# A decoder step on one core: half of a page step is put inside the projection tile ahead of it

## The reference

```python
score = jnp.einsum('bqhl,bqh->bql', jax.nn.relu(s), wi)    # s = qi . ki over all cached and new keys
_, idx = lax.top_k(score, topk)                            # 256 of 2056 keys
logits = jnp.einsum('bqhd,bqkhd->bqhk', q, ks) * HEAD_DIM ** -0.5
p = jax.nn.softmax(logits)
out = jnp.einsum('bqhk,bqkhd->bqhd', p, vs)
```

## Time and profile before

| | |
|---|---|
| runs, us | 942.56, 942.96 (median), 946.93 |
| profiled execution, us | 943.09 |
| its span, us | 941.3 |
| granted TensorE clock, mean | 0.998 |
| PE busy | 926.4 us, 98% of the span |
| DVE busy | 534.3 us, 57% |
| DMA | 205.21 MB, mean 218 GB/s |

### The profile page before, as it was taken

How to read it: one execution, slowest core, us unless ns; L and a number is a source line. 1 busy time by engine, 2 the same in 40 slices (tenths; PEclk the granted TensorE clock), 3 DMA queues, 4 the chain that set the end, 5 groups by cost and what they waited for, 6 DMA issues and landing times.

```text
span 941.3 us, 20330 instructions
## 1 busy us (share of the span) xinstructions
PE 926.4 (98%) x7052; PEld 478.3 (51%) x7064; DVE 534.3 (57%) x1625; ACT 309.5 (33%) x670; POOL 270.1 (29%) x481
## 2 busy tenths in 40 slices
PE   8999999999999999999999999999999999999996
PEld 5534444444454556654564444444445555565543
DVE  6359999579952223324354699967898323332332
ACT  3122132431242456433322221334222425563312
POOL 5832222323222222312832031323232222221130
PEclk9999999999999999999999999999999999999999
DMA  9964857677867665755885175767777667666551
GB/s 323 156 216 146 280 182 254 206 274 244 272 210 243 230 224 181 266 192 194 225 244 154 63 237 212 251 226 259 247 248 247 217 226 258 211 228 239 182 193 57
DMA packets 93665, 205.21 MB, mean 218 GB/s; under 512 B 16055, under 2 KB 28566, under 8 KB 93570
## 3 DMA queue, kind: packets, MB, share of 16 engines
q0 software_dynamic: 38576, 122.63, 38.5%
q1 hardware_dynamic: 49218, 76.87, 24.8%
q10 hardware_dynamic: 5776, 4.46, 1.8%
HBM read 193.88 MB, written 10.14 MB: 217 GB/s over the span
## 4 chain that ended last, share of the span: by engine, by line
PE 81%; DVE 10%; DMA 4%; issue 2%; ACT 1%; SPq 1%; ACTq 1%; POOL 0%; POOLq 0%; DVEq 0%
PE bank L1598 35%; PE bank L1976 12%; PE bank L1652 6%; PE bank L1581 6%; DVE r L1186 5%; PE bank L1615 4%; DMA pg<-in_cache_k_dram 4%; PE bank L1885 2%; PE bank L1848 2%; PE bank L1675 2%; PE bank L1764 2%; PE bank L1706 2%; PE bank L1894 1%; DVE sel_i L1198 1%; PE bank L1801 1%
## 5 line engine op out<-in xcount | busy, mean ns | idle before, releaser
L1598 PE MATMUL bank<-wr,ht 128*128 128x512 f32 (+1 forms) x1024 | 434.3, 577 | 0.1
L1598 PEld LDWEIGHTS bank<-wr,ht 128*128 128x128 f32 x1024 | 189.9, 190 | 212.4 <-issue 200.3
L762 POOL DMA_DIRECT2D pg<-in_cache_v_dram x128 | 69.2, 541 | 157.8 <-PE bank L1652 119.9
L762 POOL DMA_DIRECT2D pg<-in_cache_k_dram x128 | 69.4, 542 | 121.1 <-PE bank L1615 101.9
L745 POOL DMA_DIRECT2D wr<-in_w_in_dram x47 | 34.7, 738 | 234.0 <-PE bank L1598 157.5
L1186 DVE TENSOR_SCALAR_CACHE_REDUCE r<-r,sel_i 128x1088 bf16<-128x1088 f32 x62 | 83.3, 1344 | 1.7
L1615 PE MATMUL bank<-pg,qbx 128*32 128x256 f32 x1024 | 63.5, 383 | 1.9 <-DMA pg<-in_cache_k_dram 1.2
L1581 PE MATMUL bank<-wr,ht 128*32 128x256 f32 (+1 forms) x1152 | 63.6, 371 | 0.0
L1652 PE MATMUL bank<-pg,rs 128*32 128x256 f32 x1024 | 61.9, 382 | 0.1
L1976 PE MATMUL bank<-wr,qt 128*128 128x512 f32 x128 | 58.4, 599 | 0.0
L1976 PE MATMUL bank<-wr,ht 128*128 128x512 f32 x128 | 57.5, 592 | 0.0
(11 more groups left out here) (275 smaller groups left out, 1108.5 us busy)
## 6 DMA issues: line engine op xcount, KB each, us to landing
pg<-in_cache_k_dram SPq DMA_DIRECT2D x128, 256.0 KB, 5.4
pg<-in_cache_k_dram POOLq DMA_DIRECT2D x128, 256.0 KB, 5.9
pg<-in_cache_v_dram SPq DMA_DIRECT2D x128, 256.0 KB, 5.4
pg<-in_cache_v_dram POOLq DMA_DIRECT2D x128, 256.0 KB, 5.8
wr<-in_w_in_dram POOLq DMA_DIRECT2D x40, 512.0 KB, 4.2
wr<-in_w_in_dram POOLq DMA_DIRECT2D x3, 2048.0 KB, 10.4
wr<-in_w_out_dram POOLq DMA_DIRECT2D x8, 512.0 KB, 4.5
wr<-in_w_out_dram POOLq DMA_DIRECT2D x2, 2048.0 KB, 9.0
```

The costliest lines, as they stand in the source:

```text
L762: pool.dma_start(PG[2 * gi + e], cache[l, bass.ds(nos[2 * gi + e], 1), :, :].rearrange("o p n -> p (o n)"))\
L1598: mm = pe.matmul(b[0:m, 0:w], HT[:, k, rt * P:rt * P + m], W[n % 2][:, k, 0:w], start=(k == 0), stop=(k == KC - 1))
```

## The change

1. Four K steps a layer are parted: K(0,1), K(0,2), K(0,3) and K(1,2). Their half u = 0 is issued inside the tile right ahead of the step (tiles 10, 11, 12 and 17), between its k = 3 and k = 4; half u = 1 stays at the step's place.
2. `take`: the count is of scores not above the threshold, the mask is made by one subtraction, and the factor -1e30 sits in the selectors; one DVE instruction over 1088 columns goes away. The steps "rep" 0 and 1 move ahead of `take`.
3. The rotations of k, row tiles 0 to 2, move from slots 16 to 18 to behind the first three "mk" steps, in slot 18.
4. ACT's key requests of layer 0 stand in slots 0, 1, 2, 3, 3, 4, 5, 5 and no longer 0, 1, 2, 2, 3, 3, 4, 5.
5. The turning of q's row tile 3 moves one slot back, and ("sg", ST) from slot 41 to slot 43.

```diff
 SELECTORS = np.concatenate([(...) for t in range(2)], 1)
-.astype(np.float32)
+.astype(np.float32) * np.float32(-BIG)
...
-        for n, s in zip((0, 1, 2, 2, 3, 3, 4, 5), KEY_STEPS[0]):
+        for n, s in zip((0, 1, 2, 3, 3, 4, 5, 5), KEY_STEPS[0]):
...
-        if name in ("kg", "qi", "q", "k") and n != s0:
+        if name in ("kg", "qi", "q", "k") and n != s0 and (name, rt) not in (("k", 0), ("k", 1), ("k", 2)):
...
-        put(at["q", rt] + 2, FRONT, ("T", "q", rt))
+        put(at["q", rt] + 2 + (rt == 3), FRONT, ("T", "q", rt))
...
-    put(s0 + 9, FRONT, ("take",))
-    put(s0 + 10, FRONT, ("rep", 0), ("rep", 1))
+    put(s0 + 9, FRONT, ("rep", 0), ("rep", 1), ("take",))
...
+            if (p, j) == (0, 0):
+                put(n, part, *[("rope", "k", rt) for rt in range(3)])
...
-    put(41, COLS, ("sg", ST))
+    put(43, COLS, ("sg", ST))
...
+PARTED = {}
+for _l in range(DEPTH):
+    for _p, _j in ((0, 1), (0, 2), (0, 3), (1, 2)):
+        _s = ("K", _l, _p, _j)
+        PARTED[[t for t in TILE_ORDER if STEPS.index(t) < STEPS.index(_s)][-1]] = _s[1:]
...
-                then(nc.vector.tensor_scalar(SC, SC, t, None, ALU.is_gt, ALU.add, accum_out=CNT))
+                then(nc.vector.tensor_scalar(SC, SC, t, None, ALU.is_le, ALU.add, accum_out=CNT))
...
-                then(nc.vector.tensor_scalar(NEED, CNT, -1.0, float(KS_), ALU.mult, ALU.add))
+                then(nc.vector.tensor_scalar(NEED, CNT, float(KS_ - 2 * HKN), None, ALU.add))
...
-                then(nc.vector.tensor_tensor(NEED, NEED, CNT2, ALU.subtract))
+                then(nc.vector.tensor_tensor(NEED, NEED, CNT2, ALU.add))
...
-                then(nc.vector.tensor_tensor(MSK, SC, eq, ALU.add))
-                nc.vector.tensor_scalar(MSK, MSK, -1.0, BIG, ALU.add, ALU.mult).then_inc(madd_ready, 1)
+                nc.vector.tensor_tensor(MSK, SC, eq, ALU.subtract).then_inc(madd_ready, 1)
...
                     for k in range(KC):
+                        if k == KC // 2 and halfway is not None:
+                            k_step(*halfway, (0,))
                         mm = pe.matmul(b[0:m, 0:w], HT[:, k, rt * P:rt * P + m], W[n % 2][:, k, 0:w],
...
-            def k_step(l, p, j):
+            def k_step(l, p, j, halves=(0, 1)):
...
-                for u in range(2):
+                for u in halves:
...
-                    project_tile(*s[1:])
+                    project_tile(*s[1:], PARTED.get(s))
...
-                    k_step(*s[1:])
+                    k_step(*s[1:], (1,) if s[1:] in PARTED.values() else (0, 1))
```

More of the change, by code:

```diff
@@ L131 @@
 SELECTORS = np.concatenate([(((_ROW // 16) % 2 == t)[:, None] & (((_ROW // TQ) % 2)[:, None] == (_ROW // NS)[None])
-                             & ((_ROW % TQ)[:, None] == (_ROW % TQ)[None])) for t in range(2)], 1).astype(np.float32)
+                             & ((_ROW % TQ)[:, None] == (_ROW % TQ)[None])) for t in range(2)], 1).astype(np.float32) * np.float32(-BIG)
 _BIT = (1 << np.arange(BITS - 1, -1, -1)).astype(np.int32)
@@ L1584, in sample_product, with project_tile @@
                 return mm
-            def project_tile(l, name, rt):
+            def project_tile(l, name, rt, halfway=None):
                 ci, w = CHUNK[name]
```

## The result

The changed kernel takes 979.26 us (median of 6, 977.02 to 985.12; the profiled execution 978.49), the one before 944.22 (median of 6, 942.56 to 946.93). The ratio is 1.0386, 95% interval 1.0365 to 1.0407: 35 us slower, where 962.4 was forecast and 968 was the upper end. The sign and the place were right, the size was not: some 14 us, the price of a lower clock, were given to a rival with a chance of 0.08.

A forecast was written before the change was run, and what follows sets the result against it. TensorE's own list was taken as the bound, with no slack; 12.6 + 9.2 + 2.4 - 4.9 = 19.3 us on 943.09 us gives 962.4 us, 2.0% slower. Own range 957 to 968 us, 80% in 953 to 968.

The forecast's parts named there:

- The mechanism of the stops: Tiles 10, 11, 12 and 17, both layers: TensorE stops inside the tile for POOL's pages, eight stops of 2 to 4 us.
- second kind: K(0,2), K(0,3): POOL's page request stands behind the weight load's wait for the whole tile; 2.3 us four times, 9.2 us.
- first kind: K(0,1), K(1,2), both layers: the whole step ahead frees POOL's pages too late for mid-tile; 2.7 to 3.8 us each, 12.6 us.
- group 0 was out of the way: K(0,2), K(0,3): SP's pages (group 0) are requested earlier, so a landing of 5.0 us was taken for POOL's pages.
- The switch: Each parted half goes in and out of the tile once more: 0.3 us, eight times, 2.4 us; bounds 0 and 0.6.
- What it gives back: Gains across both layers: late last halves 1.8, ACT's requests 1.0, the mask 0.9, the small gate 1.2; sum 4.9 us.
- the three waits: TensorE's waits at q's turning (0.98 us), the mask's selector (0.9) and the logits behind the small gate (0.58 a layer) go.
- late last halves: Parted K steps: waits for late pages at the second half vanish, 1.8 us for five of them.
- Its expectation, 939 us: Forecast for the changed kernel with no K step parted: 944.2 - 4.9 = 939 us.
- rival (c): The clock falls behind stops; rest of tile and half a step at half speed, 18 us for four: 980 us; chance 0.08.
- PEclk under 1: Sign of being wrong: TensorE's granted clock below full in the slices of the tiles with parted halves.
- The range: Likeliest case 957 to 968 us, from second kind at 1.6 or 3.5 each (959.6 to 967.2) and switch 2.4 either way.

The follow-up runs named there:

- small moves alone: The changed kernel with no K step parted, points 2 to 5 of the change kept: 940.63 us, ratio 0.9968 to the kernel before.
- 2.87 (above): A stop in the changed kernel with only K(0,1) and K(1,2) parted, the one ending at 620.38; that kernel measured 957.25 us, ratio 1.0167.

## Why the prediction fell short

- **The mechanism of the stops.** Right, and shown: eight stops at L1626 inside the tiles named, for POOL's pages, the weight record at the tile's end and pages behind it. Asking for the pages ahead of the weights takes away the four stops of the second kind and no other. For the first kind no run makes the request earlier; there the evidence is the landing forecast from rows, and that the stops shrink as the half moves later.
- **First kind.** 12.6 us forecast, 2.9 + 2.6 + 2.9 + 3.4 = 11.8 measured. These came from rows of the same requests in the kernel before.
- **Second kind.** 9.2 forecast, 3.1 + 2.3 + 3.4 + 2.8 = 11.6 measured. The second page was issued 2.1 to 2.6 us behind the tile's end (2.2 forecast), and its landing was 5.9 us for K(0,2) and 5.5 for K(0,3), not the 5.0 taken. That group 0 was out of the way did not help enough.
- **The switch.** 0.3 us each, right.
- **What it gives back.** 3.1 of the 4.9 us were points 2 to 5 of the change; alone they measure 2.6, and the three waits went as forecast. The other 1.8, late last halves, came true too: in the changed kernel each of the eight outer halves takes 1.07 us and none waits, while the kernel without parted halves still has 1.7 us of them, read from starts. Its expectation, 939 us, took these 1.8 off by mistake; without them it is 941, and 940.6 was measured.
- **The step that failed** is the clock. The sum has no term for it; it stood only in rival (c), at 0.08, and it measures 13.9 us, more than all the other misses together. The trace of before had the clock full through waits up to 1.0 us in mid-kernel and lower behind an idle time of some 4 us, and stops of 2.3 to 3.8 us were forecast between: no row decided it, so neither outcome had grounds for 0.08, and its price belonged in the range. What the runs showed in its place: all eight stops of the profiled execution, 2.3 to 3.4 us long, were followed by products at the lower clock, and with unread products in the stops the clock stays at 1.00 and 14.0 us come back. PEclk under 1 was the prediction's own sign of being wrong. The Trainium skill's warning in "TensorE: Matmul & The Clock Gate" (Why this matters for your kernels), that idle gaps between bursts cost clock, stood beside the rival and did not raise its chance; the trace agrees with it.
- **Luck.** Rival (c)'s 980 us is close to the 979.3 measured, but not for its reasons: it priced four stops at 4.4 us each, where those four cost 6.4 us together, and left out the four of the second kind, which cost 7.5. The lower level lasts for part of what follows a stop, not for the rest of the tile and half a step.
- **The range.** By its own bounds it should have reached 969.6 (967.2 + 2.4) and not 968; the measurement lies outside either way.

The sum from the runs: 940.6 (small moves alone) + 2.7 (switches) + 23.4 (stops) + 13.9 (clock) - 1.7 (late halves gone) = 978.9; 979.3 measured.

## What to carry over

Before a piece that waits for a transfer is moved into the middle of a busy engine's work, look up when its last input *lands* and what stands ahead of the request in the issuing queue; that the old place shows no wait only says that the pages came before the old place. A stop of the bounding TensorE costs its length and the slow products behind it, here 1.4 to 2.7 us for each of eight stops; where it can't be avoided, unread products in it brought that part back. Where one edit bundles a loss with small gains, take it apart: the best kernel here is the change without its headline (940.6 us, 0.3% under the kernel before).

## Not expected of the hardware

Where the clock falls is not set by a stop's length alone. By the idle times in the profiles of all kernels here, the thirteen stops of 0.81 to 2.16 us in the kernels with the half at k = 5 and 6 left the clock at full, and all of 3.15 us and more lowered it (3.15, 3.28, 3.30, 3.35, 3.36, 3.56); between them both occur. 2.26 and 2.34 lowered it, 2.54 (half at k = 6), 2.87 (above) and, in the kernel with the halves alone, 2.21, 2.38 and even 3.13 did not:

```profile
87.60 1.07 PE L1624 MATMUL bank<-pg,qbx 128*32 128x256 f32 x16 [3.13 <-DMA pg<-in_cache_k_dram]
88.60 3.70 PE L1607 MATMUL bank<-wr,ht 128*128 128x512 f32 x8
```

When it fell it did so at the start of the inner half or only in the products behind it, and in the changed kernel it was back before the other half of the step began. So the price differs from one execution to the next: the kernel with the halves alone had the clock fall behind five stops of eight in its profiled execution, 974.98 us, the shortest of its four, and the 13.9 us above hold for one execution of the changed kernel. What decides between the two stays open; no run here bears on it.
